# The first gate's weights: low part by an adding transfer on a negative, in place of two VectorE splits

## Time and profile before

| what | value |
|---|---|
| median of 3 runs (lowest, highest) | 431.35 us (430.77, 432.27) |
| the profiled execution: its own time | 431.71 us |
| its span (first to last instruction) | 430.0 us |
| granted TensorE clock, mean of the span | 0.996 of full |
| VectorE splits (L1252) in the whole kernel | 12 of 1216 ns median |
| negatives on ScalarE (L923) | 18 of 1046 ns median |

### The profile page before, as it was taken

The page is one execution under the profiler, slowest core; times in us unless marked ns, Lnnn a source line. Parts: engine busy times, 40 slices in busy tenths (PEclk is TensorE's granted clock), DMA queues, the critical chain, the costliest instruction groups (busy, mean ns, idle before and its releaser), DMA issues.

```text
span 430.0 us, 5914 instructions
## 1 busy us (share of the span) xinstructions
PE 408.4 (95%) x2102; PEld 327.6 (76%) x2102; DVE 334.0 (78%) x554; ACT 217.5 (51%) x496; POOL 110.0 (26%) x150
## 2 busy tenths in 40 slices
PE   0899998999999998999999999999999999999996
PEld 0577785888888887778776767777788888888886
DVE  2789777599999999999989797799995996222222
ACT  3768777025211137887788989524166784100000
POOL 1400050002420443354225316973031005100000
PEclk9999998999999999999999999999999999999999
DMA  7999656306930000004003466993637059951111
GB/s 274 353 316 351 243 178 207 99 0 167 231 61 2 6 8 7 7 2 155 0 8 91 75 124 124 166 103 71 125 74 124 2 195 252 259 125 49 50 49 50
DMA packets 54327, 51.40 MB, mean 120 GB/s; under 512 B 19271, under 2 KB 49275, under 8 KB 54298
## 3 DMA queue, kind: packets, MB, share of 16 engines
q1 hardware_dynamic: 38256, 41.50, 31.0%
q0 software_dynamic: 15904, 9.44, 16.8%
q10 hardware_dynamic: 138, 0.09, 0.1%
HBM read 46.82 MB, written 4.19 MB: 119 GB/s over the span
## 4 chain that ended last, share of the span: by engine, by line
PE 54%; DVE 28%; issue 3%; ACT 2%; DMA 1%; POOL 1%; DVEq 0%; ACTq 0%
PE pm L573 7%; PE pm L574 6%; PE pm L575 6%; DVE cacc L1326 4%; PE pm L846 4%; PE pm L845 4%; PE pm L847 4%; DVE cacc L1346 3%; DVE z L1333 3%; PE tr L846 3%; PE tr L845 3%; PE tr L847 3%; PE ps L702 2%; DVE cacc L1333 2%; DVE z L1346 2%
## 5 line engine op out<-in xcount | busy, mean ns | idle before, releaser
L573 PE MATMUL pm<-h,wts 128*128 128x512 f32 x224 | 90.4, 404 | 1.3 <-DVE gb L1461 0.8
L574 PE MATMUL pm<-h,wts 128*128 128x512 f32 x224 | 87.6, 391 | 0.0
L575 PE MATMUL pm<-h,wts 128*128 128x512 f32 x224 | 87.4, 390 | 0.0
L573 PEld LDWEIGHTS pm<-h,wts 128*128 128x128 f32 x224 | 42.2, 188 | 13.4 <-issue 2.4
L575 PEld LDWEIGHTS pm<-h,wts 128*128 128x128 f32 x224 | 42.2, 188 | 9.1
L574 PEld LDWEIGHTS pm<-h,wts 128*128 128x128 f32 x224 | 42.3, 189 | 8.2 <-issue 0.2
L921 ACT ACTIVATE wts<-raw 128x1024 fp32r<-128x1024 f32 x30 | 31.2, 1051 | 33.4 <-PE pm L575 17.4
L777 PE MATMUL pm<-wts,h 128*128 128x256 f32 (+1 forms) x128 | 45.1, 352 | 0.1
L778 PE MATMUL pm<-wts,h 128*128 128x256 f32 (+1 forms) x128 | 43.1, 337 | 0.0
L779 PE MATMUL pm<-wts,h 128*128 128x256 f32 (+1 forms) x128 | 43.1, 337 | 0.0
L440 POOL DMA_DIRECT2D wts<-in_w_in x22 | 28.8, 2697 | 51.6 <-ACT wts L923 51.6
(11 more groups left out here) (209 smaller groups left out, 901.7 us busy)
## 6 DMA issues: line engine op xcount, KB each, us to landing
slab<-in_w_ada SPq DMA_DIRECT2D x16, 512.0 KB, 8.2
raw<-in_w_in SPq DMA_DIRECT2D x14, 512.0 KB, 4.9
xs<-in_x SPq DMA_DIRECT2D x8, 512.0 KB, 8.8
raw<-in_w_ada SPq DMA_DIRECT2D x8, 512.0 KB, 4.5
xr<-in_x SPq DMA_DIRECT2D x8, 512.0 KB, 5.9
out<-xr SPq DMA_DIRECT2D x15, 256.0 KB, 2.7
wts<-in_w_in POOLq DMA_DIRECT2D x6, 512.0 KB, 9.5
raw<-in_w_in SPq DMA_DIRECT2D x8, 256.0 KB, 8.0
```

The costliest lines, as they stand in the source:

```text
L573: pe.matmul(out, hi_w, hi_x, start=first, stop=False)
L574: pe.matmul(out, lo_w, hi_x, start=False, stop=False)
L575: return pe.matmul(out, hi_w, lo_x, start=False, stop=last)
```

## The change

Pieces 14 and 15 go from the one list to the other. VectorE's two splits in round 7 are gone. ScalarE writes two negatives, each right behind its high part. GpSimd issues two adding transfers at the end of its round 7, behind the root means. PE waits for their landings, and SyncE's loads of pieces 17 and 18 wait for the negatives. Of the convolution's list, two instructions are moved from round 10 to round 7. The sum of all is unchanged.

```diff
-        g_add = [sem(f"g_add{i}") for i in range(18)]
+        g_add = [sem(f"g_add{i}") for i in range(20)]
...
-        ADDED = [i for i, (u, p) in enumerate(pieces) if u in (4, 5, 8, 9, 10, 11, 12, 13, 14)]
-        LATER = [0, 1, 2, 3, 4, 5, 6, 7, 12, 13, 14, 15]
+        ADDED = [i for i, (u, p) in enumerate(pieces) if u in (4, 5, 7, 8, 9, 10, 11, 12, 13, 14)]
+        LATER = [0, 1, 2, 3, 4, 5, 6, 7, 12, 13]
...
                 if n + 1 < NT:
                     tables(n + 1)
+                if n == 7:
+                    w_lo(14)
+                    w_lo(15)
                 if n == 8:
                     w_lo(16)
...
                 if n == 10:
-                    conv(9)
+                    conv(7)
...
                     if n == 7:
-                        weights_lo(14)
-                        conv(4)
+                        conv(6)
                     else:
                         conv((4, 5, 6)[min(n, 4) - 2])
                     if b2:
                         previous_keys(b2, 1)
-                    if n == 7:
-                        weights_lo(15)
                     row_max(b2)
```

## The result

The changed kernel takes 439.13 us in the median of 6 runs (438.16 to 440.65), the one before 431.58 (430.77 to 432.27, 6 runs). The ratio is 1.0183, with a 95% interval of 1.0158 to 1.0207: 7.5 us slower, and 6.8 to 8.9 by the interval. The execution that was profiled is at the quick end: 438.16 us, with a span of 436.4.

A forecast was written before the change was run, and what follows sets the result against it. PE was taken as the bound, with about 1.1 us of air behind round 8's start. Late fifth step 5.6 plus clock 0.85 gives 6.45 us on 431.71, 438.2, less 0.36 to the median: 437.8 us (434.4 to 441.6).

The forecast's parts named there:

- clock at full price or twice: Rival: 5.6 us late fifth step plus 1.7 to 3.4 us of clock falls, 438.7 to 440.4 us; chance 0.15.
- slow transfers: Rival: landings after 8.4 us or more each, fifth step +6.9 us, same clock term, 439.1 us and up; chance 0.18.
- The bound: Behind the start of round 8 PE has about 1.1 us of air in 196, so delays there reach the end.
- fifth step: PE's fifth k-step of round 8's first gate, which wants piece 15: from 230.72 to 236.3 us, +5.6 us.
- ScalarE and POOL: Round 7: each negative costs ScalarE 0.95 us; POOL's issues at 223.96 and 229.22 put its masks at 233.5.
- The landings: Adding transfers of pieces 14 and 15 land 7.1 us after issue, at 231.06 and 236.3; bounds 3.5 and 8.4.
- The clock: PE's idleness around round 8 brings one clock fall, costing 0 or 1.7 us; 0.85 us taken.
- quick transfers: Rival: landings take 3.5 us, fifth step 2.0 us late, 433.4 us (433.1 by the skill's formula); chance 0.09.
- Not slower: Rival at PE's wait before the fifth step: piece 15 lands about 2 us after issue, giving 431.1 us; chance 0.06.
- DVE's relief: Two splits, 2.5 us of DVE, removed; in round 10 it wins nothing, as the 2.94 us mask wait only grows.

The follow-up runs named there:

- a4_neg_only: The kernel before, with ScalarE also writing the negatives of pieces 14 and 15, which VectorE's splits overwrite; no adding transfer: 433.55 us, ratio 1.0053.
- c4_change_again: The changed kernel with no edit, run once more on the chip of some other versions: 437.53 us, ratio 1.0163.
- a3_only15: The changed kernel, but only piece 15 gets its low part by the adding transfer, piece 14 by VectorE's split: 438.15 us, ratio 1.0173.
- c1_hold_both: The changed kernel, but SyncE's loads of pieces 17 and 18 both wait for the second adding transfer's landing: 436.81 us, ratio 1.0124.
- b2_hold_loads: The changed kernel, but SyncE's loads of pieces 17 and 18 wait for the landings of adding transfers 14 and 15 respectively: 440.46 us, ratio 1.0196.
- a1_conv_back: The changed kernel, with the two convolution instructions left in round 10 as before: 439.50 us, ratio 1.0191.

## Why the prediction was right

It said 437.8 us (434.4 to 441.6), slower with 0.93; measured 439.13. The mechanism is the one that was forecast: two waits for landings, and a lateness that stays to the end. The second landing was mis-sized, and so was what a fall of the clock can cost at most. The number alone would also fit two of the rivals: it lies within "clock at full price or twice" (438.7 to 440.4) and at the edge of "slow transfers" (439.1 and up). The landings in the profile decide against the second; how near the runs around the median come to the first is left open below. Point by point:

- **The bound.** "Whatever holds PE up there comes out at the end nearly one for one." In nine of the fourteen profiles the clock did not fall behind the fifth step. In eight of them the rest is 199.25 to 199.50 us, whether the fifth step came at 8.66 or at 15.38; the ninth, a4_neg_only with 199.91, has another wait behind it. This was the step that carried the forecast, and it held to 0.25 us.
- **ScalarE and POOL.** Negatives at 222.6 and 227.9, issues at 224.0 and 229.2, masks done at 233.5: the trace has 222.68, 227.92, 224.02, 229.26 and 233.08 + 0.41. The transposes moved to 226.65 as worked out.
- **The landings.** Taken 7.1 for both, measured 7.0 and 7.7. The term of the fifth step was therefore put at 5.6 and came to 6.37 in the profiled execution (the start of `w_hi(14)` differs by 0.05). In thirteen transfers of these two pieces in the other profiles that had loads beside them the landing took 6.9 to 8.1. The term was mis-sized because one row was taken for a constant. And to price SyncE's loads at "nothing" was wrong. Nobody waits for them, but they cost the two transfers 1 to 2 us: alone these land after 6.0 to 6.2 us. (Piece 16's 7.1 had such a load beside it, so the sum held that price without naming it.)
- **The clock.** 0.85 us was taken, the middle of 0 and 1.7, as a stand-in for not knowing where the fall comes. The profiled execution paid 0, c4_change_again 1.5. What the median paid was not measured apart. Of the 1.33 us by which 437.8 fell short, 0.23 is the kernel before (431.35 in three runs, 431.58 in six) and 0.77 the fifth step; the 0.33 left would be the clock at 1.2 instead of 0.85. That is a remainder. It fits with the three runs next to the median, whose spans are 437.3 to 437.4 us at the same mean clock (0.996) as the profiled 436.4: they lost about 1 us that this one did not. Where their fall lay no trace shows. The bound of 1.7 for one fall was too low: a3_only15 lost 2.6.
- **The rival of quick transfers** fell. No adding transfer of 512 KB landed in under 6.0 us in any profile. The estimate of 3.2 us by the formula in the Trainium skill, "DMA: Bandwidth & Descriptors", section "Anatomy of one DMA — SWDGE (gpsimd) path", does not hold for an adding transfer of this shape, even alone (6.0 to 6.2 us); in c1_hold_both the moving itself took over 3 us of that.
- **The rival of slow transfers** (8.4 or more each) was not seen either: 7.0 and 7.7 in the profiled execution, and 8.1 at most for these two pieces in any other.
- **Not slower** would have needed a landing by about 2 us. None was seen.
- **DVE's relief** was worth nothing, as said: its wait for masks at the end of round 10 grew from 2.94 to 4.44 us in the changed kernel,

```profile
283.95 0.76 DVE L1336 SCALAR_TENSOR_TENSOR z<-z,cw 128x513 f32<-128x513 f32 x1 [4.44 <-POOL pcur L483]
```

and PE's two waits of 0.8 us stayed.

What stays open: why one landing is 7.0 and another 8.1 with the same neighbours; what decides, run by run, on which side of the second wait the clock falls; and how much of the median's 7.5 us is the clock's.

## What to carry to other kernels

Before work is moved from an engine to a transfer, compare two dates: when the reader wants the data, and when its last input is ready plus the issue and the landing. Here the input is ready 3.7 to 5.2 us ahead of the reader, a split takes 1.2 us and a transfer 6 to 8, and 2.5 us less work on an engine that isn't the bound did not outweigh that. Of the two late pieces only the last date counted; and a transfer that nobody waits for still lengthens the one beside it that somebody does wait for.

## What the runs showed of the hardware

- An adding transfer of 512 KB issued by GpSimd lands 6.0 to 6.2 us after the start of its issue with no load beside it (five transfers in three kernels), and 6.9 to 8.1 with SyncE's loading of one piece beside it (fifteen transfers; the piece comes as one load of 512 KB or as four of 128 KB). A plain load of 512 KB by SyncE landed in 5.9 us beside such a transfer (b2_hold_loads).
- A fall of TensorE's clock behind the last of the two waits cost 1.5 to 2.6 us (the rest in five profiles against before's), and one between the two waits cost nothing in three profiles (changed, a1_conv_back, c1_hold_both), because the second wait absorbed it. Filling only the first wait gained nothing.
- A fall of the clock near 70 us, far from the changed place, comes in some executions and not in others (five of fourteen profiles). The runs of the kernel before fall into two groups by their mean clock, some 1.9 us apart (spans near 429.1 and 431.0 us on one chip); a difference of a few tenths of a us can be looked for only within a group.
